# State-space block: where the second group's projection slabs stand between the first group's outputs, and where its silus stand between the exponentials

## The reference, cut to what matters

```python
c = jax.nn.silu(centred_dwconv(conv_in, conv_w, conv_b))          # x, B, C of both groups
cs = jnp.cumsum(dt * A.reshape(G, Hg), axis=2)
Lmat = jnp.exp(jnp.where(incl, cs[:, :, :, None] - cs[:, :, None, :], -jnp.inf))
cb = jnp.einsum('bnigs,bnjgs->bnijg', Cm, Bm)
y_intra = jnp.einsum('bnijgh,bnjghp->bnighp', cb[..., None] * Lmat, xdt)
...
y = y_fw + y_bw + ssd_D.astype(F32)[:, None] * x_ssd
y = y.reshape(Bsz, L, SSD_WIDTH) * jax.nn.silu(z)
```

## Time and profile before

| | us |
|---|---|
| median of 3 runs | 3797.08 |
| lowest and highest | 3796.36 and 3808.59 |
| profiled execution, its time | 3804.26 |
| profiled execution, span of its instructions | 3802.2 |
| mean granted PE clock of it | 0.942 of full speed |

### The profile page before, as it was taken

The page is one execution under the profiler, slowest core; times in us unless marked ns, Lnnn a source line. Parts: engine busy times, 40 slices in busy tenths (PEclk is TensorE's granted clock), DMA queues, the critical chain, the costliest instruction groups (busy, mean ns, idle before and its releaser), DMA issues. The chain is left out here.

```text
span 3802.2 us, 39200 instructions
## 1 busy us (share of the span) xinstructions
PE 3369.6 (89%) x15418; PEld 2427.8 (64%) x15418; DVE 1732.8 (46%) x2515; ACT 1037.4 (27%) x1473; POOL 244.7 (6%) x212
## 2 busy tenths in 40 slices
PE   4988899977868775999998889998999998889997
PEld 3464755634655223888784568887888784568886
DVE  2668575655642003443326644433443326644433
ACT  2121211212321003322214543222322214542222
POOL 1100100011110001000002000000000002000001
PEclk6999999988978997999999899999999998899998
DMA  2110010010213991322211013222322301022221
GB/s 76 56 34 22 23 45 23 12 56 1 89 58 152 421 420 48 110 99 98 102 45 61 1 67 110 99 92 76 107 92 100 111 34 61 1 75 103 99 100 55
DMA packets 50689, 326.30 MB, mean 86 GB/s; under 512 B 7040, under 2 KB 7424, under 8 KB 13056
## 3 DMA queue, kind: packets, MB, share of 16 engines
q1 hardware_dynamic: 50560, 324.52, 22.9%
HBM read 321.35 MB, written 2.10 MB: 85 GB/s over the span
## 5 line engine op out<-in xcount | busy, mean ns | idle before, releaser
L364 PE MATMUL psum<-ffn_x_hi,ffn_w_hi 128*128 128x512 f32 x1408 | 548.3, 389 | 1.5 <-DVE ffn_x_lo L320 1.3
L364 PE MATMUL psum<-ffn_x_hi,ffn_w_lo 128*128 128x512 f32 x1408 | 547.8, 389 | 0.0
L364 PE MATMUL psum<-ffn_x_lo,ffn_w_hi 128*128 128x512 f32 x1408 | 547.8, 389 | 0.0
L309 DVE TENSOR_TENSOR ffn_w_lo<-ffn_raw,ffn_w_hi 128x2048 fp32r<-128x2048 f32 x128 | 293.4, 2292 | 421.4 <-ACT ffn_w_hi L280 421.4
L104 PE MATMUL psum<-mix_normed,mix_ring 128*128 128x512 f32 x832 | 377.5, 615 | 41.6 <-DVE recurrences_work L654 22.3
L280 ACT ACTIVATE ffn_w_hi<-ffn_raw 128x2048 fp32r<-128x2048 f32 x128 | 245.3, 1916 | 566.0 <-PE psum L364 565.2
L104 PEld LDWEIGHTS psum<-mix_normed,mix_ring 128*128 128x128 f32 x832 | 163.5, 198 | 250.6 <-issue 240.8
L364 PEld LDWEIGHTS psum<-ffn_x_hi,ffn_w_hi 128*128 128x128 f32 x1408 | 264.4, 188 | 61.6 <-DVE ffn_w_lo L316 6.7
L364 PEld LDWEIGHTS psum<-ffn_x_hi,ffn_w_lo 128*128 128x128 f32 x1408 | 264.3, 188 | 55.1
L364 PEld LDWEIGHTS psum<-ffn_x_lo,ffn_w_hi 128*128 128x128 f32 x1408 | 264.4, 188 | 54.4
L364 PE MATMUL psum<-ffn_hid_hi,ffn_w_hi 128*128 (+1 forms) x704 | 273.9, 389 | 0.0
(11 more groups left out here) (471 smaller groups left out, 5339.8 us busy)
## 6 DMA issues: line engine op xcount, KB each, us to landing
ffn_raw<-w_ffn SPq DMA_DIRECT2D x128, 1024.0 KB, 4.8
mix_ring<-w_experts SPq DMA_DIRECT2D x48, 1024.0 KB, 13.6
mix_ring<-w_mix SPq DMA_DIRECT2D x32, 1024.0 KB, 7.1
mix_normed<-w_experts SPq DMA_DIRECT2D x24, 1024.0 KB, 13.6
experts_slabs<-w_experts SPq DMA_DIRECT2D x24, 1024.0 KB, 13.6
mix_ring<-w_gdn SPq DMA_DIRECT2D x16, 1024.0 KB, 4.8
mix_ring<-w_ssd SPq DMA_DIRECT2D x10, 1024.0 KB, 4.8
mix_ring<-w_out SPq DMA_DIRECT2D x7, 1024.0 KB, 7.7
```

Of the source, the lines that this page charges most:

```text
L309: dve.tensor_tensor(w_lo[:, q, :], raw[:, q, :], w_hi[:, q, :].bitcast(F32), ALU.subtract)\
L364: ins = pe.matmul(out, wp[:, q, w], xp, start=start and a == 0, stop=stop and a == 2)
```

## The change

Three queues are written in another order; no instruction of the computation is added or taken away, and no semaphore or wait is changed.

```diff
 # PE
-            for j in range(1, 5):
-                for n in range(4 * j, 4 * j + 4) if j < 4 else ():
-                    decay(0, n)
-                if j < 4:
-                    tiles(j + 1)
-                outputs(0, j - 1)
+            for n in range(4, 8):
+                decay(0, n)
+            tiles(2)
+            outputs(0, 0)
+            for n in range(8, 12):
+                decay(0, n)
+            outputs(0, 1)
+            tiles(3)
+            for n in range(12, 16):
+                decay(0, n)
+            outputs(0, 2)
+            tiles(4)
+            outputs(0, 3)
 # ACT
-            for n in (6, 7, 0, 1):
+            for n in (6, 7):
                 silu(n)
-            exps(0, range(0, 8))
-            for n in (2, 3):
-                silu(n)
-            exps(0, range(8, 12))
-            for n in (4, 5):
+            exps(0, range(0, 12))
+            for n in (0, 1, 2, 3):
                 silu(n)
             exps(0, range(12, 16))
-            for n in (8, 9):
+            for n in (4, 5, 8, 9):
                 silu(n)
 # DVE
             scores(0, range(8, 12))
+            out(0, 1)
             conv(4)
-            out(0, 1)
             scores(0, range(12, 16))
```

## The result

The changed kernel takes 3781.9 us in the median of five runs (3778.62 to 3783.11). The kernel before takes 3797.08, now also of five (3795.19 to 3808.59). The ratio over all these runs is 0.9947, with a 95% interval of 0.9933 to 0.9962, so the changed kernel is faster by 14 to 25 us. The medians alone are 15.2 us apart, and the two profiled executions 3804.26 - 3782.07 = 22.2 us. The forecast was 3766.6 us. The direction and what was said of the three waits were right, but only half to three quarters of the 30.5 us foretold arrived: a wait came that the forecast did not have.

What follows compares the result with a forecast made beforehand. PE, 89% busy, was taken to bound the kernel, idling for ACT's late exponentials. Pieces summing to 82.92 us instead of 113.40 gave 30.5 off the 3797.08 median: 3766.6 us, range 3760 to 3780.

Steps and rivals of the forecast that it cites:

- The three waits go, and the slow starts with them: PE, decay 0 to output 3: waits for ACT (22.99 us) and slow decays after them (7.41 us) vanish.
- Slab 4 is the tightest place, with 1.6 us to spare: PE's slab 4 at 877.4 waits for slab 3's convolution, done on DVE at 875.8; no wait expected.
- Table loads: ACT: decay 0's load runs ahead of its wait, free; decay 12's costs 0.21 us, making four decays 7.35.
- the item on the 16 products: DVE's products of decays 0 to 7, at 0.68 to 1.53 us each, delay slab 3 by 0 us, at worst 0.7.
- The forecast's own signs: PE from decay 0: no bracket over 1 us, no decay over 2 us, slabs at 14.3, 41.7 and 66.0 us.
- The rival that the slow clock stays: PE's waits go but the lower clock remains, so only 22.99 us are gained: 3774.1 us; chance 0.10.
- all decays slow: All PE decays run at the lower clock, 28.6 us more: 3795.2 us, no change; chance 0.03.
- slower: PE's unbroken stretch is not granted full speed, up to 82.9 us more: 3849.5 us; chance 0.03.
- The wait moves: PE's wait for ACT only moves to exponential 8, behind output 0, with its slow start: 3797 us; chance 0.04.

Runs made afterwards that it cites:

- e1_yield: The changed kernel, with DVE waiting for POOL's right sides of decays 6 and 7 before its products of decays 0 and 1: 3770.95 us, ratio 0.9919.
- e11_one_wait: The changed kernel, with DVE waiting before its first product until POOL has made decay 6's right side: 3763.8 us in 2 runs, ratio 0.9911.
- e10_one_psum: The changed kernel, with the third of DVE's 12 products reading from PSUM, its exponential left out of the result: 3773.16 us, ratio 0.9939.

## Why the prediction was right in part

- *The three waits go, and the slow starts with them*: shown. PE has no wait for ACT, and with POOL let in the stretch is 30.7 us shorter (e1_yield) against 30.48 foretold. It was ACT's order that did it, though; the forecast gave the three orders together and did not say so. The lengths hold: slab 2 takes 847.28 - 833.45 = 13.83, decays 12 to 15 with the reload 881.83 - 874.60 = 7.23 instead of 7.35.
- *Slab 4 is the tightest place, with 1.6 us to spare*: it had 1.5. The convolutions beside POOL were not slowed (12 instructions in 7.96 us).
- *Table loads*: the first ran ahead of its wait, as argued. The Trainium skill, "ScalarE: Activation LUTs", section "What ACT_TABLE_LOAD costs", puts about 1.38 us of draining on top of each switch. The trace does not agree: the last exponential of decay 11 ends at 858.26, the load starts at 858.28, and the first silu starts 1.29 us behind that. Decay 12 with its load took 7.23 us for four decays, less than the 7.35 of the sum; but ACT had idled 13.94 us before it, so the row above is the better test.
- *The step that failed* is the item on the 16 products, "I take 0: POOL has only a few instructions there". The forecast's own signs point at it: a bracket over 1 us (6.60), and decays over 2 us (two in 5.41). Slabs 2, 3 and 4 began 22.5, 49.8 and 74.1 us behind decay 0 instead of 14.3, 41.7 and 66.0, each about 8 us late. I priced the meeting of DVE and POOL on DVE's side alone, since the earlier trace rows show DVE as the one who is late. A decay has two waits, for ACT to have read its banks and for POOL's right side; the second was never laid against the timetable. Its term was set at 0 and measured 6.60 us of waiting and 1.84 of slow decays, 8.44 of the 30.48. The kernel before did not show it: in group 0 its products came behind their exponentials, and where DVE had a run in group 1, POOL got in. The change lets ACT run ahead while DVE convolves, so 12 products were ready at once, just as POOL was on the path.
- *The rival that the slow clock stays* (3774.1) came nearer to the median than the forecast did, but by luck: the clock was 1.00 until the wait for POOL and low only in it and behind it, and the slow starts behind the old waits were gone. Of the rivals "all decays slow" and "slower" the traces show nothing: from 833.4 to 902.2 the clock was 1.00. "The wait moves" named the right kind of thing but the wrong engine.
- *The range* ended at 3780, below the median of 3781.9. It held no term for a wait that the old trace could not show; from the earlier trace rows POOL's delay was at least 1.39 - 1.05 = 0.34 us, and nothing in the rows bounded it from above short of DVE's whole run.

## What to carry to other kernels

When a wait goes, an engine that had worked in small pieces behind it may get all its work at once; look at who shares SBUF access with it, and price the meeting for both sides. If a long run of DVE instructions with two SBUF inputs stands beside a POOL instruction on the path, put a wait for POOL ahead of the run (e11_one_wait: 8.5 us of the stretch) or try a PSUM-reading instruction in it (e10_one_psum: 7.8 us, in a kernel whose result left something out). Before moving pieces on the engine that waits, try the order of the engine that is waited for alone: here it was the whole gain, and moving PE's pieces by themselves cost 3.6 us of the stretch.

## What the runs showed of the hardware that was not expected

POOL's product of 128x512, usually 1.05 us and up to 1.60 beside DVE, took 8.18 us beside 12 DVE products of two SBUF inputs that followed the convolution without a gap, 4.57 beside six, and 1.05 beside 12 that read one operand from PSUM. In group 1 it took 2.60 in three of the 13 profiles, held by the last two products of a run. A held POOL came free when the run ended, or when an instruction with a PSUM input began.

What makes such a run hold POOL is open. In group 0, a gap of about 1 us before the run (e11_one_wait), or work that becomes ready piece by piece, let POOL in at the next product, and then DVE's product took 1.53. I had thought that DVE's queue is filled ahead while it convolves. That was not tried by itself, and it does not explain group 1, where DVE had been busy for some 30 us and POOL was held in three profiles and let in in ten.
